# Banded attention by half tiles, and each V row's engine from a count of the work around its step

## The chip, the cores and the metric

The kernel runs on one core of a Trainium2 chip. The metric is the device time of one execution in microseconds (us). A measurement of before is a median of three executions.

## What is computed

One layer of a streaming encoder on 1024 tokens of width 1024, in float32: a norm, one input projection, two token mixers in parallel (gated linear attention; attention in a sliding band with sinks and distance slopes), their gated sum and projection, then a retrieval layer with product keys, a gated per-layer embedding, and a last norm. The two parts that the change touches are these:

```python
CHUNK = 64; SWA_WINDOW = 128          # a chunk of queries sees its own chunk and the one before
def swa_branch(q, k, v, sinks):
    ...
    logits = jnp.einsum('bnqhgd,bnkhd->bnhgqk', qc, kb).astype(f32) * (SWA_HEAD_DIM ** -0.5)
    ...
    dist = jnp.abs((W - 1) * CHUNK + qi[:, None] - kj[None, :]).astype(f32)
    logits = logits - slopes[:, :, None, None] * dist
    ...
    probs = jax.nn.softmax(jnp.concatenate([logits, sink], axis=-1), axis=-1)[..., :-1]
    out = jnp.einsum('bnhgqk,bnkhd->bnqhgd', probs.astype(v.dtype), vb)

def peer_ffn(h, w_q, sub_keys, u_tab, v_tab):
    ...   # for each token and each of 8 heads: the 16 best of 16384 experts, and their gates
        u = jnp.take(u_tab, e, axis=0)
        act = jax.nn.gelu(jnp.einsum('td,thkd->thk', xt, u).astype(f32))
        vv = jnp.take(v_tab, e, axis=0)
        return jnp.einsum('thk,thkd->td', (g * act).astype(xt.dtype), vv)
```

## The kernel before

**Rows.** Tokens lie in 8 tiles of 128. For each tile, head and rank one "row" of the retrieval layer is one indirect gather by GpSimd (L554): for 128 tokens the expert's u and v vectors, side by side, 8 KB a token, 1 MB in all. There are 1024 rows, and `uv` is a ring of ten. VectorE multiplies the u half with the token (`dot`, L1303, into `dots`), ScalarE makes the gelu (L1039) and the weight (L1044), and then the v half is added to the tile's sum, in one of two ways. Either VectorE does it (`add_row`, L1331, into `acc`), or ScalarE writes the weights as a diagonal matrix (`diagonal`, L1053, three buffers) and TensorE adds the row in PSUM by matmuls of 512 columns (L789, into `ysum`). `IS_PE` says which. Before, it holds a fixed pattern for each tile: every third row of a head's 16 for tiles 0 and 1, every second for tiles 2 to 5, three of four for tiles 6 and 7. The first six rows of a tile and the last four of all are VectorE's. GpSimd issues the gather of a row when the row ten before it is used, by the one engine or the other.

**Steps.** A step is two rows; there are 512 in which gathers are used (0 to 511), and negative ones for the opening. In step n VectorE does the dots of step n and two pieces of the top-k of a later head, then its rows of step n - 1. ScalarE makes the weights of step n - 1 and the diagonals of step n - 2, and TensorE adds its rows of step n - 2.

**Stages.** All the rest is cut into stages, which `plan()` puts on steps, for five segments of 1, 1, 2, 2 and 2 tiles: `gk`, `gv`, `gq`, `gr`, `sk`, `sv`, `sq` (projections), `la`, `u0`, `o0`, `t0` (linear attention), `lg`, `ex`, `va` (banded attention), `bgg`, `glo`, `bgs`, `swo`, `wo` (gates and output), `wq1` to `wq8` (queries and key search), and a tail `T0` to `T2` for finished tiles. Most of them begin with a weight slab of 1 MB, of which three fit; its matmuls (L597, L607) are a "piece". Each engine runs its own program in order: TensorE does a stage in its step, ScalarE and VectorE in the next. In a step TensorE does its due rows ahead of the stage. TensorE's results go through two PSUM banks that ScalarE empties (`copied`, L822), and TensorE waits for a bank to be emptied before it fills it again.

**Banded attention.** A batch is one tile with two groups of four heads (8 heads); a tile has two. `lg` multiplies 128 queries with 192 keys (three chunks, of which each query may see two, L646); VectorE adds slope times distance, where the table `dist` has 1e33 for keys that a query may not see, and takes the maximum (`biased`, L1120, L1124). `ex` has ScalarE's exponentials (L865) and VectorE's division (L1137). In `va` TensorE turns the probabilities, padded to 256 columns, in blocks of 128 (L660), ScalarE copies them out, and TensorE multiplies with V of two blocks (L666).

## Time and profile before

| | us |
|---|---|
| median of 3 executions | 3538.31 |
| lowest, highest | 3530.22, 3539.45 |
| the profiled execution, its time | 3534.93 |
| its span | 3533.1 |
| TensorE busy (share of the span) | 2829.1 (80%) |
| VectorE busy | 2572.2 (73%) |
| ScalarE busy | 1409.4 (40%) |
| GpSimd busy | 1287.0 (36%) |

In the profile PE is TensorE, PEld its weight loads, DVE VectorE, ACT ScalarE, POOL GpSimd and SP SyncE. The page shows the span in 40 equal slices: a digit is a busy share in tenths, GB/s is what the DMA engines moved. A row of the view by windows reads: from and to (us), length, busy time of PE, PEld, DVE, ACT and POOL (each with its number of instructions), the granted clock of TensorE as a share of 2.4 GHz, the DMA engines' mean busy share, and GB/s. The chain of waits is the work that ended last, followed back; a row is start, length, engine, what it wrote and its line. A matmul in float32 is two records, a transpose one.

### The profile page before, as it was taken

How to read it: one execution, taken by the hardware profiler on the slowest of the kernel's cores; microseconds unless marked ns; L12 is line 12 of the kernel's file. 1: busy time of each engine (PE TensorE's matmuls, PEld its weight loads, DVE VectorE, ACT ScalarE, POOL GpSimd, SP SyncE). 2: the span in 40 equal slices, each digit the busy share in tenths (PEclk: the TensorE clock that was granted, in tenths of full speed). 3: DMA queues.
4: the chain of work that ended last, by engine and by line, in shares of the span. 5: the costliest groups of instructions: out<-in, count | busy, mean ns of one | idle time of the engine just before them, and what ended most of it. 6: DMA issues, size and time to landing. Idle time of an engine off the chain costs nothing.

```text
span 3533.1 us, 35079 instructions
## 1 busy us (share of the span) xinstructions
PE 2829.1 (80%) x11044; PEld 1910.4 (54%) x11044; DVE 2572.2 (73%) x5366; ACT 1409.4 (40%) x3568; POOL 1287.0 (36%) x1028
## 2 busy tenths in 40 slices
PE   8889788987787997777876879978895978657665
PEld 7777566755565865444544637655473635213223
DVE  0247668798878868888777996787768885776664
ACT  2324543434433343444333443444534335334332
POOL 0012233343433244444442443343333433544441
PEclk9999899999998999898987989989998989879887
DMA  6589899999999999999999999999999999999995
GB/s 239 171 313 420 355 416 421 421 401 391 371 405 404 375 390 421 421 416 417 421 421 377 422 409 421 419 419 398 375 406 419 417 390 383 420 421 421 421 422 216
DMA packets 195915, 1376.57 MB, mean 390 GB/s; under 512 B 22401, under 2 KB 24321, under 8 KB 32018
## 3 DMA queue, kind: packets, MB, share of 16 engines
q0 software_dynamic: 147456, 1073.81, 74.0%
q1 hardware_dynamic: 48274, 300.51, 21.4%
q8 instruction: 90, 1.47, 0.2%
q14 instruction: 95, 0.78, 0.1%
HBM read 1363.22 MB, written 11.01 MB: 389 GB/s over the span
## 4 chain that ended last, share of the span: by engine, by line
PE 38%; DMA 28%; DVE 16%; issue 8%; ACT 6%; POOL 2%; DVEq 0%; POOLq 0%; SPq 0%; ACTq 0%
DMA uv<-in_uv,idx 24%; PE bank L597 14%; PE bank L607 10%; PE ysum L789 8%; DVE acc L1331 4%; DVE uv L1303 4%; DMA slab<-in_slabs 3%; POOL uv L554 2%; PE bank L666 2%; DVE lidx L1156 1%; DVE vals L1153 1%; ACT bufX L865 1%; DMA out<-bufA 1%; PE bank L660 1%; DVE bufE L1150 1%
## 5 line engine op out<-in xcount | busy, mean ns | idle before, releaser
L554 POOL DMA_INDIRECT uv<-in_uv,idx x1024 | 1286.8, 1257 | 2189.3 <-PE ysum L789 1004.4
L1303 DVE SCALAR_TENSOR_TENSOR uv<-uv,hbuf 128x1024 f32<-128x1024 f32 x1024 | 1244.8, 1220 | 420.5 <-DMA uv<-in_uv,idx 402.2
L789 PE MATMUL ysum<-uv,diag 128*128 128x512 f32 x2004 | 1059.1, 670 | 417.4 <-ACT diag L1053 412.2
L789 PEld LDWEIGHTS ysum<-uv,diag 128*128 128x128 f32 x2004 | 405.3, 212 | 937.0 <-ACT diag L1053 524.2
L1331 DVE SCALAR_TENSOR_TENSOR acc<-uv,dots,acc 128x1024 f32<-128x1024 f32 x523 | 668.9, 1279 | 107.8 <-ACT dots L1044 91.5
L1039 ACT ACTIVATE dots<-dots 128x2 f32<-128x2 f32 x512 | 102.9, 201 | 1017.2 <-DVE uv L1303 1011.5
L597 PE MATMUL bank<-bufA,slab 128*128 128x256 f32 (+1 forms) x2400 | 440.3, 343 | 14.3 <-DMA slab<-in_slabs 11.0
L597 PEld LDWEIGHTS bank<-bufA,slab 128*128 128x128 f32 x2400 | 391.4, 195 | 84.4 <-issue 32.9
L607 PE MATMUL bank<-slab,bufA 128*128 128x256 f32 x1408 | 317.7, 385 | 7.3 <-DMA slab<-in_slabs 4.7
L607 PEld LDWEIGHTS bank<-slab,bufA 128*128 128x128 f32 x1408 | 270.3, 193 | 61.3 <-issue 17.6
L597 PE MATMUL bank<-bufC,slab 128*128 128x256 f32 (+1 forms) x1280 | 245.0, 353 | 28.7 <-DMA slab<-in_slabs 14.2
L597 PEld LDWEIGHTS bank<-bufC,slab 128*128 128x128 f32 x1280 | 217.8, 204 | 71.1 <-issue 44.6
L1044 ACT ACTIVATE dots<-dots,gexp 128x1 f32<-128x1 f32 x1024 | 245.9, 287 | 20.6
L1039 ACT ACT_TABLE_LOAD x160 | 205.3, 1283 | 2.8
L1053 ACT ACTIVATE diag<-ident,dots 128x128 f32<-128x128 f32 x501 | 192.7, 395 | 11.9 <-PE ysum L789 5.5
L822 ACT ACTIVATE bufE<-bank 128x512 f32<-128x512 f32 (+1 forms) x136 | 69.6, 519 | 299.1 <-PE bank L597 272.0
L607 PE MATMUL bank<-slab,bufC 128*128 128x256 f32 x512 | 118.4, 391 | 15.4 <-DMA slab<-in_slabs 10.0
L666 PE MATMUL bank<-bufX,sv 128*64 128x512 f32 x128 | 81.8, 773 | 59.1 <-ACT bufX L822 59.1
L597 PE MATMUL bank<-bufQ,slab 128*128 128x256 f32 (+1 forms) x640 | 117.5, 343 | 4.0 <-DMA slab<-in_slabs 4.0
L607 PEld LDWEIGHTS bank<-slab,bufC 128*128 128x128 f32 x512 | 99.7, 196 | 37.9 <-DMA slab<-in_slabs 13.3
L607 PE MATMUL bank<-slab,bufQ 128*128 128x256 f32 x512 | 115.7, 385 | 2.2 <-ACT bufE L822 1.5
L597 PE MATMUL bank<-bufB,slab 128*128 128x256 f32 (+1 forms) x640 | 116.6, 341 | 0.0
(146 smaller groups left out, 2425.7 us busy)
## 6 DMA issues: line engine op xcount, KB each, us to landing
slab<-in_slabs SPq DMA_DIRECT2D x255, 1024.0 KB
uv<-in_uv,idx POOLq DMA_INDIRECT x1024
x_d<-acc SPq DMA_DIRECT2D x7, 512.0 KB
bufA<-in_x SPq DMA_DIRECT2D x3, 1024.0 KB, 11.8
bufA<-x_d SPq DMA_DIRECT2D x3, 1024.0 KB
out<-bufA SPq DMA_DIRECT2D x3, 1024.0 KB, 12.1
bufE<-in_g_ffn SPq DMA_DIRECT2D x5, 512.0 KB, 9.5
bufX<-in_g_fin SPq DMA_DIRECT2D x5, 512.0 KB
```

Source lines behind the costliest of these rows:

```text
L554: nc.gpsimd.indirect_dma_start(out=uv[:, at % NS, :], out_offset=None, in_=a["uv"], in_offset=bass.IndirectOffsetOnAxis(ap=idx[:, g % 4, k ...
L597: m = mm(o, w[:, k, g * P:g * P + P], src(k), start=(k == 0), stop=(k == KT - 1))
L607: m = mm(b[:, c0:c0 + PW], src[:, k, t * P:t * P + P], w[:, k, :], start=(k == 0), stop=(k == KT - 1))
L660: m = nc.tensor.transpose(b[:, c0:c0 + P], probs[:, GROUP * e + 2 * half + j, blk * P:blk * P + P], ident[:])
L666: m = mm(b[r0:r0 + HD, :], sv[:, t + blk, g * HD:g * HD + HD], pT[:, :, blk, :], start=(blk == 0), stop=(blk == 1))
L789: ins = mm(ysum[:, c, :], diag[:, m % DS, :], uv[:, at % NS, D + c * 512:D + c * 512 + 512], start=(m == first), stop=(m == last))
L822: fn(dst, src, kw.pop("func", ACT.Copy), **kw).then_inc(emptied, 1)
L1039: fn(part, part, ACT.Gelu_apprx_tanh).then_inc(gelu_done, 1)
L1044: m = fn(dots[:, g % 3, k:k + 1], dots[:, g % 3, k:k + 1], ACT.Copy, scale=gexp[:, g % 4, k:k + 1])
L1053: fn(diag[:, m % DS, :], ident[:], ACT.Copy, scale=dots[:, g % 3, k:k + 1]).then_inc(diag_done, 1)
L1303: v.scalar_tensor_tensor(out=row, in0=row, scalar=1.0, in1=hbuf[:, i % HB, :], op0=ALU.mult, op1=ALU.mult, accum_out=dots[:, g % 3, k:k + ...
L1331: v.scalar_tensor_tensor(out=row, in0=uv[:, at % NS, D:2 * D], scalar=dots[:, g % 3, k:k + 1], in1=row, op0=ALU.mult, op1=ALU.add).then_in ...
```

## The change

`BAND` becomes two chunks. In `lg` each half of a tile (64 queries) gets its own 128 keys, so a head is two matmuls of 64 rows by 128 columns, and no key is outside the band but for the first tile's missing chunk. Probabilities are 8 blocks of 128 columns without padding, so a head is one transpose and not two, and a group's turned probabilities take one bank and not two. V is held twice: `sv` as before, and `sv0` shifted by a chunk, which ScalarE fills with two more copies when it empties the bank of stage `sv`. `values` multiplies the first half's queries with `sv0` and the second half's with `sv`, 256 columns each, where two matmuls of 512 columns were summed up.

`IS_PE` comes from `shared_rows()`. It goes through the steps with a count for TensorE and one for VectorE, in a unit of its own: each is lowered by a step's pace (385, and 190 for a slab), raised by the stages' work from a table, and a row goes to the engine whose count is the lower with it. Rows of TensorE's are 586 after and 501 before; by tile 30, 56, 72, 78, 68, 66, 104, 112 after, and 38, 38, 61, 61, 61, 61, 92, 89 before. The plan of the stages is the same.

```diff
-BAND = 3 * CHUNK
+BAND = 2 * CHUNK
...
-ON_PE = [SOME, SOME, ODD, ODD, ODD, ODD, MOST, MOST]
...
-IS_PE = [at % TOPK in ON_PE[at // (NH * TOPK)] and at % (NH * TOPK) >= SPARE and at < ROWS - 4
-         for at in range(ROWS)]
...
+def work(s, n):
+
+    tt = tiles_in(s, n)
+    kind = n.rstrip("0123456789")
+    scores = kind == "wq" and n != "wq0"
+    pe = {"pp": 270 * tt, "hT": 95 * tt, "hb": 95 * tt, "T1": 200 * tt, "ga": 170 * tt + 100, "la": 75 * tt, "u": 270,
+          "o": 270, "t": 170 + 270 * (n[-1] != str(tt - 1)), "lg": 220, "va": 400}.get(kind, 0)
+    if n in PIECES and n != "pp":
+        pe += 535 if tt > 1 else 280 if kind in ("gk", "gv", "gr", "wo", "pg", "sv") else 345
+    dve = {"ga": 50 * tt, "la": 50 * tt, "u": 300, "o": 165, "t": 300 * (n[-1] != str(tt - 1)), "lg": 300, "ex": 120,
+           "glo": 30 * tt, "swo": 60 * tt, "rt": 110 * tt, "mx": 155 * tt}.get(kind, 0)
+    if n in ("wo3", "T2"):
+        dve += 100 * tt
+    return pe + 45 * tt * scores, dve + 230 * tt * scores
+
+
+def shared_rows():
+
+    found = []
+    pe = dve = 0
+    for n in range(END):
+        now, last = AT_STEP.get(n, []), AT_STEP.get(n - 1, [])
+        pace = 385 + 190 * sum(name in PIECES for _, name in now)
+        pe = max(pe - pace, 0) + sum(work(*stage)[0] for stage in now)
+        dve = max(dve - pace, 0) + 260 + sum(work(*stage)[1] for stage in last)
+        for at in (2 * n, 2 * n + 1):
+            may = at % (NH * TOPK) >= SPARE and at < ROWS - 4
+            found.append(may and pe + 135 < dve + 100)
+            if found[-1]:
+                pe += 135
+            else:
+                dve += 100
+    return found
...
     if n[:2] == "va":
-        return 6
+        return 4
...
                     for j in range(GROUP):
-                        o = wide[:, 2 * e + j // 2, (j % 2) * BAND:(j % 2) * BAND + BAND]
-                        m = mm(o, sqT[r0:r0 + HD, (g // 2) * GROUP + j, t * P:t * P + P],
-                               skT[r0:r0 + HD, g // 2, t * P:t * P + BAND], start=True, stop=True)
+                        for q0 in (0, CHUNK):
+                            m = mm(wide[q0:q0 + CHUNK, e, j * BAND:j * BAND + BAND],
+                                   sqT[r0:r0 + HD, (g // 2) * GROUP + j, t * P + q0:t * P + q0 + CHUNK],
+                                   skT[r0:r0 + HD, g // 2, t * P + q0:t * P + q0 + BAND], start=True, stop=True)
...
-                    for half in range(2):
-                        b = bank_for()
-                        for j in range(2):
-                            for blk in range(2):
-                                c0 = (2 * j + blk) * P
-                                m = nc.tensor.transpose(b[:, c0:c0 + P], probs[:, GROUP * e + 2 * half + j,
-                                                                              blk * P:blk * P + P], ident[:])
-                        m.then_inc(bank_full, 1)
+                    b = bank_for()
+                    for j in range(GROUP):
+                        m = nc.tensor.transpose(b[:, j * P:j * P + P], probs[:, GROUP * e + j, :], ident[:])
+                    m.then_inc(bank_full, 1)
                     pe.wait_ge(emptied, used.n)
-                    b = bank_for()
-                    for blk in range(2):
-                        m = mm(b[r0:r0 + HD, :], sv[:, t + blk, g * HD:g * HD + HD], pT[:, :, blk, :],
-                               start=(blk == 0), stop=(blk == 1))
+                    b = bank_for()[r0:r0 + HD, :].rearrange("p (j n) -> p j n", j=GROUP)
+                    for half, of in ((0, sv0), (1, sv)):
+                        q = slice(half * CHUNK, half * CHUNK + CHUNK)
+                        m = mm(b[:, :, q], of[:, t, g * HD:g * HD + HD], pT[:, :, q], start=True, stop=True)
                     m.then_inc(bank_full, 1)
...
                 elif n == "sv":
-                    rows(sv[:, 1:TT + 1, :], 0, tt)
+                    for ts in token_banks(tt):
+                        b = full()[:, 0:len(ts) * PW].rearrange("p (t n) -> p t n", t=len(ts))
+                        fn(sv0[0:CHUNK, ts[0] + 1:ts[-1] + 2, :], b[CHUNK:P], ACT.Copy)
+                        fn(sv0[CHUNK:P, ts[0]:ts[-1] + 1, :], b[0:CHUNK], ACT.Copy)
+                        copied(sv[:, ts[0]:ts[-1] + 1, :], b)
```

How it moves instructions shows in the listing of TensorE's program. The first place is the opening, tile 0's first batch: logits, two gates' pieces, then for each of two groups the transposes and the values. Before:

```order
L646 MATMUL wide<-skT,bufQ 128x192 x8
L597 MATMUL bank<-bufA,slab 128x128 x32
L660 MATMUL bank<-ident,bufX 128x128 x8
L666 MATMUL bank<-bufX,sv 64x512 x2
L660 MATMUL bank<-ident,bufX 128x128 x8
L666 MATMUL bank<-bufX,sv 64x512 x2
```

and after:

```order
L680 MATMUL wide<-skT,bufQ 64x128 x16
L631 MATMUL bank<-bufA,slab 128x128 x32
L692 MATMUL bank<-ident,bufX 128x128 x4
L698 MATMUL bank<-bufX,sv 64x4x64 x2
L692 MATMUL bank<-ident,bufX 128x128 x4
L698 MATMUL bank<-bufX,sv 64x4x64 x2
```

Twice as many logits of two thirds the columns; half the transposes; values of half the columns (the listing names `sv` for both copies of V).

The second place is segment 2, steps 80 to 84: a piece of `glo`, batch 1's values, a piece of a gate, batch 2's logits, and the V rows between them (`ysum<-uv,diag`, two matmuls a row). Before:

```order
L597 MATMUL bank<-bufB,slab 128x256 x16
L660 MATMUL bank<-ident,bufX 128x128 x8
L666 MATMUL bank<-bufX,sv 64x512 x2
L660 MATMUL bank<-ident,bufX 128x128 x8
L666 MATMUL bank<-bufX,sv 64x512 x2
L789 MATMUL ysum<-uv,diag 128x512 x2
L597 MATMUL bank<-bufA,slab 128x256 x16
L646 MATMUL wide<-skT,bufQ 128x192 x8
L789 MATMUL ysum<-uv,diag 128x512 x4
```

and after:

```order
L631 MATMUL bank<-bufB,slab 128x256 x16
L820 MATMUL ysum<-uv,diag 128x512 x4
L692 MATMUL bank<-ident,bufX 128x128 x4
L698 MATMUL bank<-bufX,sv 64x4x64 x2
L692 MATMUL bank<-ident,bufX 128x128 x4
L698 MATMUL bank<-bufX,sv 64x4x64 x2
L631 MATMUL bank<-bufA,slab 128x256 x16
L680 MATMUL wide<-skT,bufQ 64x128 x16
L820 MATMUL ysum<-uv,diag 128x512 x2
```

The row between the values and the gate's piece is gone, and two rows stand ahead of the values.

The third place is tile 6's part of the program, steps 407 to 411, with the tail of finished tiles: transposes (`T1`), then pieces of `pg`. Before:

```order
L586 MATMUL bank<-ident,bufB 128x128 x16
L789 MATMUL ysum<-uv,diag 128x512 x6
L607 MATMUL bank<-slab,bufQ 128x256 x16
L789 MATMUL ysum<-uv,diag 128x512 x6
L607 MATMUL bank<-slab,bufQ 128x256 x16
```

and after:

```order
L620 MATMUL bank<-ident,bufB 128x128 x16
L820 MATMUL ysum<-uv,diag 128x512 x8
L641 MATMUL bank<-slab,bufQ 128x256 x16
L820 MATMUL ysum<-uv,diag 128x512 x4
L641 MATMUL bank<-slab,bufQ 128x256 x16
```

Between two pieces stood three rows, and now two stand there.

## Rows read from the trace of the kernel before

**Rows 1.** The page: slices of DMA share and rate, and the gathers' queue.

```profile
DMA  6589899999999999999999999999999999999995
GB/s 239 171 313 420 355 416 421 421 401 391 371 405 404 375 390 421 421 416 417 421 421 377 422 409 421 419 419 398 375 406 419 417 390 383 420 421 421 421 422 216
...
q0 software_dynamic: 147456, 1073.81, 74.0%
```

**Rows 2.** The view by windows, the stretches of the span that the prediction counts.

```profile
90.00:146.00 56.00, 44.24 (x271) 32.83 (x270) 14.19 (x34) 23.96 (x61) 0.00 (x0) 0.88 0.38 130
146.00:249.00 103.00, 90.05 (x659) 84.57 (x658) 29.99 (x127) 25.20 (x59) 9.52 (x10) 0.93 0.77 277
...
371.00:431.00 60.00, 50.85 (x301) 37.18 (x302) 34.87 (x62) 28.47 (x67) 11.94 (x10) 0.86 0.82 325
431.00:737.00 306.00, 267.58 (x1311) 210.97 (x1310) 231.15 (x492) 123.46 (x291) 107.72 (x86) 0.94 1.01 420
737.00:1060.00 323.00, 262.92 (x1019) 184.18 (x1017) 269.47 (x474) 140.19 (x362) 123.87 (x96) 0.92 0.97 389
...
1138.00:1294.00 156.00, 143.69 (x588) 111.03 (x589) 121.68 (x304) 56.47 (x131) 49.20 (x40) 0.95 0.93 367
...
1900.00:2066.00 166.00, 137.48 (x508) 94.54 (x508) 150.97 (x433) 66.84 (x163) 66.46 (x55) 0.91 0.97 391
...
2390.00:2600.00 210.00, 183.03 (x674) 120.99 (x673) 158.21 (x295) 96.94 (x255) 74.49 (x63) 0.95 0.96 385
...
2830.00:3010.00 180.00, 144.16 (x425) 80.22 (x423) 126.24 (x277) 79.43 (x195) 73.24 (x58) 0.90 0.97 387
3010.00:3488.00 478.00, 312.50 (x608) 128.26 (x608) 328.17 (x608) 165.53 (x479) 216.38 (x174) 0.85 1.01 419
3488.00:3533.00 45.00, 19.14 (x74) 14.94 (x72) 12.80 (x14) 12.39 (x25) 0.00 (x0) 0.75 0.10 37
```

**Rows 3.** Who waited for whom at 871 to 880 us: total, times, longest.

```profile
DVE acc L1331 <- ACT dots L1044: 7.6, 1, 7.6
ACT L859 <- PE bank L597: 7.5, 1, 7.5
POOL uv L554 <- PE ysum L789: 7.4, 1, 7.4
```

**Rows 4.** The chain of waits, tile 0's first batch in the opening.

```profile
92.93 2.25 PE wide L646 x16
95.19 3.78 PE bank L597 x32
...
100.93 3.61 ACT bufX L865 x16
...
105.11 1.77 DVE bufX L1137
...
106.98 1.56 PE bank L660 x8
...
109.22 3.67 PE bank L666 x4
112.89 1.74 PE bank L660 x8
...
115.30 1.93 PE bank L666 x4
```

**Rows 5.** Groups by line, VectorE: dots, and rows into `acc`.

```profile
L1303 DVE SCALAR_TENSOR_TENSOR uv<-uv,hbuf 128x1024 f32<-128x1024 f32 x1024 | 1244.8, 1220 | 420.5 <-DMA uv<-in_uv,idx 402.2
...
L1331 DVE SCALAR_TENSOR_TENSOR acc<-uv,dots,acc 128x1024 f32<-128x1024 f32 x523 | 668.9, 1279 | 107.8 <-ACT dots L1044 91.5
```

**Rows 6.** The chain of waits: a row of TensorE's twice, and a piece.

```profile
385.07 1.72 PE ysum L789 x4
...
846.12 3.78 PE ysum L789 x4
...
2940.25 6.91 PE bank L607 x32
```

More of the change, by code:

```diff
@@ L180 @@
     AT_STEP.setdefault(_at, []).append((_s, _n))
+SPARE = 6
+def work(s, n):
[27 more added lines that the diff above has]
+    return found
+IS_PE = shared_rows()
+PE_UPTO, DVE_UPTO = [0], [0]
+for _at in range(ROWS):
+    PE_UPTO.append(PE_UPTO[-1] + IS_PE[_at])
+    DVE_UPTO.append(DVE_UPTO[-1] + (not IS_PE[_at]))
 def feature_banks(tt):
@@ L873, in window_out @@
                     r0 = (g % 2) * HD
[L874 to L876 removed]
+                    copied(pT, full().rearrange("p (j n) -> p j n", n=P))
                     copied(yswT[r0:r0 + HD, (g // 2) * GROUP:(g // 2) * GROUP + GROUP, t * P:t * P + P],
```

39 lines of the change are left out of this document (13 added, 26 removed).

## The prediction

> **What bounds the kernel now.** I read the page's slices first. From the fourth slice to the last but one the DMA engines are 80 to 100% busy and move 421 or 422 GB/s at the most, in 12 of the 40 slices just that [rows 1]. 74.0% of 16 engines' span is the 1024 gathers of expert rows [rows 1]; weight slabs are most of the rest. The change moves no byte of either (the table of distances alone shrinks, by 64 KB). So the kernel is bound by a transfer that it can't shorten, and what a change of the engines' work can give is only the time in which the transfer doesn't run at 421 GB/s.
>
> Next I cut the span into stretches and counted for each its length times (421 - GB/s)/421. At 431 to 737 us it is nothing (420 GB/s), at 3010 to 3488 us 2 us [rows 2]. What is left lies in three places. **The opening**, before gathers fill the engines, runs far below the rate up to 249 us, and 56 us of it, where tile 0's attention lies, at 130 GB/s [rows 2]. **Six stretches** in the middle lose 13.7 (371 to 431), 24.6 (737 to 1060), 20.0 (1138 to 1294), 11.8 (1900 to 2066), 18.0 (2390 to 2600) and 14.5 us (2830 to 3010), together 102.6 us [rows 2]. **The end**, 45 us after the last gathers at 37 GB/s [rows 2], holds tile 7's last norm and isn't touched.
>
> What makes a loss? The waits at 871 to 880 us show one whole [rows 3]: GpSimd waits 7.4 us for a row's matmul to free a slot of the ring of ten; VectorE waits 7.6 us for the weights that ScalarE makes; and ScalarE stands 7.5 us on a sigmoid, for TensorE to end the slab piece before it. Each engine runs its program in order, so a TensorE that is one piece late stops the other three, and the ring runs dry. Such a loss is a backlog of TensorE or VectorE in the steps with stages, larger than the ring's lead. A step's own budget is the transfer's: two rows are 2.1 MB, 5.0 us at 421 GB/s, and a slab adds 2.5 us.
>
> **The attention part.** The chain of the opening gives its prices, since there one batch (8 heads of a tile) stands on the chain link by link [rows 4].
> - Logits: 2.25 us for 16 records of 192 columns become 32 records of 128 columns in tiles of 64 rows by 64 columns. No row of before has that form. From above: 32 records of 128 columns in a slab piece took 3.78 us [rows 4], so +1.5. From below: if the two halves lay over each other, 1.9, so -0.35. I take +1.5, the form's nearest row. The Trainium skill (TensorE: Matmul & The Clock Gate, Part 3: Packing small matmuls) says that matmuls at different tile positions run at the same time; the two query halves differ in position, so by it the lower end would hold, and the sum below would be 4 us better in the opening. No run here shows such a pair yet.
> - Exponentials: eight in 3.61 us, each a third narrower. Between 0 and -1.2; I take -0.4, as most of an operation so short is fixed.
> - Normalizing: 1.77 us for 1536 elements, 1024 now: -0.6.
> - Transposes: half as many, 1.56 and 1.74 us: -1.65.
> - Values: columns halved, 3.67 (the low clock) and 1.93 us: -2.8. The eviction between transposes and values stays on the chain; the one that goes lay beside transposes.
> - Bias and maximum on VectorE become a third shorter too; they lie beside a gate's slab piece of 3.78 us. I count nothing; were that cover gone, 1.2 us more a batch.
>
> Sum: 3.95 us a batch on the chain, 7.9 us for the opening's two. Against it stand two more ScalarE copies where the V slab's bank is emptied (sv0's halves; TensorE's second next bank waits for them), under 1 us in the opening: I take 0.4. The opening gives **7.5 us**, with ends of 4 and 13. Since the gathers fill the DMA engines right behind it, nothing else can eat this.
>
> **The rows' engines.** A row costs VectorE 1.28 us and TensorE 1.72 at the full clock (3.4 for two), 3.78 at the low one [rows 5, 6]; a step's two dots cost VectorE 2.4 us [rows 5], and its top-k pieces are the same before and after. Before, TensorE has 501 of 1024 rows, dealt evenly within a tile; after, 586. The 85 that move take 109 us off VectorE and put 146 us on TensorE, neither of which is at its limit over the span, so the number matters little; where they lie does. In the listing of TensorE the piece, the row, the piece become the piece, the piece, and then four or eight matmuls of rows. With 2-tile pieces (6.91 us [rows 6]) and a row a step, TensorE needed 8.6 us of 7.5 in a stage step and 1.7 of 5.0 in an empty one; now 6.9 and 3.4. VectorE with both rows needs 5.0 of 7.5 and top-k, without them 2.4 of 5.0.
>
> Stretch by stretch, what of the loss goes:
> - 371 to 431: one-tile stages, two a step, two attention batches. The rows of steps 13 to 20 go from 5 on TensorE to 1 (7 us), and the batches give 8 us of chain. TensorE's lag here was its own work; of 13.7 I take **9**.
> - 737 to 1060: four batches, TensorE's rows 28 to 37 of 96. VectorE had 269.5 us busy of 323 [rows 2] with its bias, states and gates in bursts; it loses 9 rows (11.5 us) and 4 x 1.9 us of attention; the pairs now lie off the stages. Of 24.6 I take **16**.
> - 1138 to 1294: key search (two lists a tile) and the next segment's slabs together, no attention. TensorE is busy 143.7 of 156 us, VectorE 121.7 [rows 2]. There is no spare engine to move to: 16 rows become 15. Only the backlog that VectorE brings along from the steps ahead is smaller (7 of 20 rows on TensorE become 13). Of 20.0 I take **7**.
> - 1900 to 2066: the same search with tile 0's and 1's tail between; rows 24 to 32 of 54. Of 11.8 I take **6**.
> - 2390 to 2600: three batches, 12 us of chain. But rows run on TensorE two steps behind their gather, and here stages lie in two steps of three, so the pairs that were put on empty steps run in stage steps after all: 19 rows in its 13 steps with pieces, where 13 were. Of 18.0 I take **10**.
> - 2830 to 3010: tile 6, where 3 of 4 rows were TensorE's and its pieces came on top; Rows that run in a piece's step fall from 12 to 3 (15 us). Of 14.5 I take **11**.
>
> Together **59 of 102.6 us**; the ends are 25 and 98. Quiet stretches gain nothing: they run at the transfer's rate already.
>
> **The sum.** The profiled execution took 3534.9 us (its span 3533.1). 3534.9 - 7.5 - 59 = 3468.4. It lies 3.4 us under the median shown, so I forecast **3470 us**.
>
> **Rivals.**
> *The convoy stays.* The losses may come less from too much work than from the hand-overs (TensorE to ScalarE to VectorE and back), which the change leaves as they are, each batch still passing from engine to engine over six times. Then only the shorter batches count: some 25 us of the six stretches and the opening's 7.5: **3505**. For it: in [rows 3] nobody was overloaded within the 8 us themselves. Against: TensorE came late there after values that get shorter and a row that goes.
> *All stalls go.* If a loss needs a backlog over some threshold and the even load stays under it, 95 us go: **3435**. For it: 431 to 737 us, with as many stages a step, lost nothing. Against: the stretch at 1138.
> *The low clock (slower).* With pairs in every quiet step (166 of 178 rows at 3010 to 3488 us, 129 before) TensorE needs 3.4 us of 5.0 at 2.4 GHz, but 7.6 at 1.2 GHz [rows 6], where the transfer sets 5.0. The granted clock there is 0.85 on the mean [rows 2], so it spends about three tenths of the time at 1.2 GHz already. Each pair step held at 1.2 GHz with no slack left costs 2.6 us; there are 83. From 26 of them (67 us) the whole gain is eaten; half of them held give **3575**. For it: engines that pause between pairs are what rows show at the lower clock. Against: a TensorE that falls behind stops pausing, and in the stretches where it never paused the clock was full (2830 to 3010: 0.90; 371 to 431, with long waits, 0.86 [rows 2]); the ring's lead covers some steps. The Trainium skill names the same danger (TensorE: Matmul & The Clock Gate, table on what matters for kernels): idle gaps between bursts bring half the rate. By it the matmuls of a pair run slow; whether steps do is what the price above says.
> *It does not do what it says.* The planner's counts don't shift rows by the two steps at which TensorE runs them, so loads could rise where they should fall, and new stalls cancel the gain: **3530**.
>
> **How the numbers follow.** Forecast (3448 to 3490) 0.50; the convoy (3490 to 3520) 0.22; all stalls go 0.16; cancelled 0.06; the low clock 0.06. The range 3428 to 3512 leaves out the last two and the upper part of the second. A measurement can tell 0.3%, 11 us: faster than 3528 has 0.89, the same 0.05, slower 0.06.
>
> **What would show it.** Right: the first dot starts 7 to 8 us earlier; 371 to 431, 737 to 1060 and 2830 to 3010 at over 405 GB/s, 1138 to 1294 still under 400; values' matmuls half as long; a page with the same bytes. Wrong: waits of GpSimd for ysum of over 7 us in quiet stretches with the clock under 0.8 (the low clock), or the six stretches still losing over 70 us with engines less busy (the convoy).

## The result, and the profile after

| | us |
|---|---|
| after, median of 6 executions | 3510.7 |
| lowest, highest | 3507.9, 3518.2 |
| before, beside it | 3537.1 |
| after's profiled execution, its span | 3508.0, 3506.2 |

The change is faster by 0.7%: 0.993 of before, with a 95% interval of 0.991 to 0.994. That is 26 us where 67 were forecast. The time lies at the very end of the range (3512), near the rival "the convoy stays" (3505) and not at the forecast. That it lies inside at all is luck: it comes by a sum that neither the forecast nor a rival had.

The page of after (each engine's busy time, share and instructions; GB/s in 40 slices of the span; the gathers' queue with packets, MB and share):

```profile
PE 2874.4 (82%) x11512; PEld 1941.1 (55%) x11512; DVE 2458.6 (70%) x5276; ACT 1420.2 (41%) x3631; POOL 1236.4 (35%) x1028
...
GB/s 240 200 315 414 372 417 421 421 410 413 401 401 403 397 421 421 421 408 408 421 421 344 422 382 421 421 421 400 418 416 407 408 389 393 421 421 421 421 421 214
...
q0 software_dynamic: 147456, 1073.81, 74.3%
```

Against [rows 1] the bytes are the same, and the shape too: the same full stretches, the same dips. Some dips are shallower (401 to 403 where 371 to 375 stood) and one is deeper (344 where 377 stood). VectorE lost 114 us of work and TensorE gained 45, as the moved rows and the smaller attention make it. Busy time says little here: the transfer sets the pace.

To compare like with like, the spans are cut at the first dot of the same steps, not at the same microseconds, and the loss of each stretch is counted as the prediction does: length times (421 - GB/s)/421. The view by windows of after, so cut, with the columns of [rows 2]; the steps are 0 to 20, 63 to 110, 111 to 143, 144 to 242, 243 to 275, 323 to 356, 357 to 392, 393 to 421, and the quiet ones from 422:

```profile
243.00:420.00 177.00, 138.95 (x929) 116.38 (x927) 131.26 (x266) 84.45 (x199) 49.95 (x39) 0.91 0.96 393
...
728.00:1041.00 313.00, 259.13 (x1066) 184.32 (x1065) 251.61 (x463) 137.33 (x362) 120.91 (x95) 0.90 0.99 405
1041.00:1268.00 227.00, 212.80 (x887) 160.21 (x886) 187.54 (x514) 94.63 (x217) 79.53 (x66) 0.97 0.99 404
1268.00:1850.00 582.00, 481.04 (x1689) 300.60 (x1688) 433.95 (x823) 237.94 (x657) 245.51 (x201) 0.93 1.01 417
1850.00:2066.00 216.00, 169.46 (x573) 107.74 (x572) 175.04 (x499) 86.03 (x212) 77.32 (x66) 0.90 0.93 374
...
2361.00:2564.00 203.00, 176.12 (x704) 119.02 (x704) 164.23 (x310) 94.28 (x255) 78.36 (x66) 0.92 1.00 410
2564.00:2807.00 243.00, 198.88 (x742) 141.90 (x743) 184.57 (x471) 90.50 (x223) 82.73 (x73) 0.90 1.00 410
2807.00:2983.00 176.00, 139.84 (x407) 77.55 (x406) 126.50 (x275) 79.60 (x194) 71.68 (x60) 0.90 0.96 391
2983.00:3456.00 473.00, 344.11 (x744) 143.83 (x744) 283.79 (x567) 175.76 (x512) 191.26 (x173) 0.93 1.01 421
```

The same table for before and for the kernels of the experiments, in us of loss (each from the profiled execution of its kernel):

| steps | before | after | att_only | rows_only | t1_undo | t1_pairs | search_old | mix | mix2 | ring9 | shifted | lag1 |
|---|---|---|---|---|---|---|---|---|---|---|---|---|
| 0-20 | 13.9 | 11.8 | 9.7 | 23.5 | 14.0 | 9.2 | 15.0 | 9.3 | 10.2 | 21.2 | 14.1 | 3.4 |
| 21-62 | 0.7 | 0.7 | 0.0 | 1.5 | 0.7 | 0.0 | 2.2 | 3.6 | 0.0 | 2.2 | 0.7 | 0.0 |
| 63-110 | 24.6 | 11.9 | 20.5 | 15.8 | 9.6 | 15.6 | 10.3 | 10.4 | 7.9 | 17.2 | 17.1 | 19.2 |
| 111-143 | 19.3 | 9.2 | 23.1 | 9.2 | 9.2 | 19.2 | 9.2 | 7.5 | 9.4 | 14.5 | 10.0 | 15.0 |
| 144-242 | 1.4 | 5.5 | 1.4 | 14.0 | 6.9 | 0.0 | 5.5 | 2.8 | 4.2 | 14.0 | 11.2 | 36.0 |
| 243-275 | 11.7 | 24.1 | 12.7 | 22.0 | 18.6 | 16.5 | 10.4 | 12.7 | 12.2 | 27.8 | 9.5 | 18.6 |
| 276-322 | 0.0 | 0.0 | 1.4 | 0.0 | 0.0 | 2.1 | 0.0 | 0.7 | 0.7 | 0.7 | 2.1 | 0.0 |
| 323-356 | 18.3 | 5.3 | 7.0 | 13.0 | 6.3 | 7.6 | 6.3 | 3.5 | 6.5 | 10.5 | 5.3 | 18.6 |
| 357-392 | 1.1 | 6.3 | 0.5 | 11.7 | 5.8 | 2.8 | 2.8 | 1.1 | 2.8 | 14.9 | 5.2 | 16.2 |
| 393-421 | 14.4 | 12.5 | 15.2 | 11.6 | 14.7 | 16.2 | 14.2 | 14.1 | 10.2 | 18.8 | 8.0 | 33.7 |
| sum | 105.3 | 87.4 | 91.6 | 122.2 | 85.8 | 89.1 | 76.1 | 65.6 | 64.0 | 141.9 | 83.2 | 160.7 |

After against before: 23 us go at steps 63 to 143 and 13 at 323 to 356, but 12 come at 243 to 275, 4 at 144 to 242 and 5 at 357 to 392. So more than half of what went in one place came back in another. The row of before for steps 243 to 275, against that of after above (1850 to 2066 us):

```profile
1883.00:2088.00 205.00, 153.66 (x527) 99.42 (x525) 188.23 (x513) 82.14 (x200) 82.62 (x65) 0.84 0.98 397
```

A caution for all that follows: stretches whose program is the same in two kernels still differ by up to 5 us (steps 63 to 110: 20.5 and 15.6 in att_only and t1_pairs), and att_only's profiled execution (3511.4) was the slowest of its own, 8.5 us above its median. Medians decide between kernels; the table tells only where.

The opening went about as forecast in size. After's first dot starts at 243.0 us, before's at 249.4. In the profiles of all twelve kernels with the new attention it starts between 239.1 and 243.9, so the single 6.4 us stands for 5.5 to 10. The chain of waits of after, tile 0's first batch (start, us, what):

```profile
93.08 1.52 PE wide L680 x32
94.60 3.78 PE bank L631 x32
...
100.34 3.19 ACT bufX L896 x16
...
104.10 1.24 DVE bufX L1169
...
105.44 1.13 PE bank L692 x4
...
107.24 1.97 PE bank L698 x4
109.20 1.06 PE bank L692 x4
...
110.94 1.97 PE bank L698 x4
```

Held against [rows 4]: the logits took 0.7 us less, not 1.5 more (and less than the lower end, 0.35 less); exponentials 0.4 less; normalizing 0.5 less; the two lots of transposes 1.1 less; the values 1.7 less. From the first logit to the last value the batch went from 24.3 to 19.8 us.

### The profile page after: what moved, and what is told of

The parts are those of the page before. It is cut to its first block, busy times and chain, and to the rows that moved or that the text cites. A ratio compares the mean times of both kernels' runs of the same rounds, so it can differ in the third digit from the quotient of the medians.

```text
span 3506.2 us, 36073 instructions
## 1 busy us (share of the span) xinstructions
PE 2874.4 (82%) x11512; PEld 1941.1 (55%) x11512; DVE 2458.6 (70%) x5276; ACT 1420.2 (41%) x3631; POOL 1236.4 (35%) x1028
## 4 chain that ended last, share of the span: by engine, by line
PE 38%; DMA 33%; DVE 13%; ACT 7%; issue 6%; POOL 2%; DVEq 0%; SPq 0%; ACTq 0%; POOLq 0%
DMA uv<-in_uv,idx 28%; PE bank L631 14%; PE ysum L820 12%; PE bank L641 8%; DMA slab<-in_slabs 4%; DVE uv L1335 4%; DVE acc L1363 3%; POOL uv L588 2%; PE bank L698 1%; DVE lidx L1188 1%; DVE vals L1185 1%; ACT bufX L860 1%; ACT bufX L896 1%; ACT dots L1077 1%; PE bank L620 1%
## 5 line engine op out<-in xcount | busy, mean ns | idle before, releaser
L588 POOL DMA_INDIRECT uv<-in_uv,idx x1024 | 1236.2, 1207 | 2209.8 <-PE ysum L820 1335.8
L820 PE MATMUL ysum<-uv,diag 128*128 128x512 f32 x2344 | 1155.0, 640 | 342.1 <-ACT diag L1086 330.8
L820 PEld LDWEIGHTS ysum<-uv,diag 128*128 128x128 f32 x2344 | 462.3, 204 | 928.3 <-issue 500.7
L1363 DVE SCALAR_TENSOR_TENSOR acc<-uv,dots,acc 128x1024 f32<-128x1024 f32 x438 | 561.1, 1281 | 73.4 <-ACT dots L1077 51.4
L641 PE MATMUL bank<-slab,bufA 128*128 128x256 f32 x1408 | 322.8, 390 | 11.9 <-ACT bufA L882 6.2
L631 PE MATMUL bank<-bufC,slab 128*128 128x256 f32 (+1 forms) x1280 | 241.2, 350 | 14.1 <-ACT bufA L882 6.7
L1086 ACT ACTIVATE diag<-ident,dots 128x128 f32<-128x128 f32 x586 | 211.3, 394 | 49.6 <-PE ysum L820 41.8
L853 ACT ACTIVATE bufE<-bank 128x512 f32<-128x512 f32 (+1 forms) x136 | 69.8, 519 | 318.0 <-PE bank L631 279.2
L641 PE MATMUL bank<-slab,bufC 128*128 128x256 f32 x512 | 123.0, 402 | 27.2 <-DMA slab<-in_slabs 14.5
L631 PE MATMUL bank<-bufQ,slab 128*128 128x256 f32 (+1 forms) x640 | 119.3, 346 | 14.4 <-DMA slab<-in_slabs 13.8
L631 PEld LDWEIGHTS bank<-bufQ,slab 128*128 128x128 f32 x640 | 104.9, 195 | 30.9 <-DMA slab<-in_slabs 16.0
## 6 DMA issues: line engine op xcount, KB each, us to landing
out<-bufA SPq DMA_DIRECT2D x3, 1024.0 KB, 11.7
```

What stands on the lines that cost most here:

```text
L588: nc.gpsimd.indirect_dma_start(out=uv[:, at % NS, :], out_offset=None, in_=a["uv"], in_offset=bass.IndirectOffsetOnAxis(ap=idx[:, g % 4, k ...
L631: m = mm(o, w[:, k, g * P:g * P + P], src(k), start=(k == 0), stop=(k == KT - 1))
L641: m = mm(b[:, c0:c0 + PW], src[:, k, t * P:t * P + P], w[:, k, :], start=(k == 0), stop=(k == KT - 1))
L820: ins = mm(ysum[:, c, :], diag[:, m % DS, :], uv[:, at % NS, D + c * 512:D + c * 512 + 512], start=(m == first), stop=(m == last))
L853: fn(dst, src, kw.pop("func", ACT.Copy), **kw).then_inc(emptied, 1)
L1086: fn(diag[:, m % DS, :], ident[:], ACT.Copy, scale=dots[:, g % 3, k:k + 1]).then_inc(diag_done, 1)
```

## Experiments

All kernels compute the whole layer. Edits are against after unless it says otherwise. Differences in us are between medians. Before was measured again beside each group: 3535.4 beside att_only, rows_only, diag6 and search_old, 3536.2 beside lag1, att_lag1, shifted and mix, 3537.7 beside t1_undo, t1_pairs, ring9 and mix2, against 3537.1 beside after. So a difference of a few us between two groups says little; the ratios, given with their 95% intervals, are each to the before beside them.

**Halves of the change: att_only and rows_only.** The first has the new attention with the old rows, the second the old attention with the new rows:

```diff
-IS_PE = shared_rows()
+IS_PE = [at % TOPK in ON_PE[at // (NH * TOPK)] and at % (NH * TOPK) >= SPARE and at < ROWS - 4
+         for at in range(ROWS)]
```

> The new attention with the old fixed shares of rows (501 on TensorE). Theory A (the gain is the shorter batches; the new shares give back what they win, because a row of TensorE's is freed a step later than one of VectorE's): 3537 less the opening's 6 us and some 15 to 25 us of the six stretches, 3506 to 3516, so as fast as the whole change (3511) or faster. Rival B (the shares bring half of the gain and more): 3520 to 3530.

> The old attention with the new shares, the same rows on the same engines as in the changed kernel (586). Theory A: little, 3530 to 3545; the loss of steps 247 to 252 and 379, which grew with the change, shows here as well (7 us and 4 us more than before), the steps 335 to 343 get better. Rival B: 3515 to 3522.

att_only: 3502.9 us, 0.991 (0.990 to 0.993). rows_only: 3547.8 us, 1.003 (1.002 to 1.005). The attention alone is worth 34 us (32.5 against the before beside it), more than the whole change; the rows alone make the kernel 11 to 12 us slower. Each lies some 3 us outside what theory A said, and rival B is out. Put on the new attention the new shares cost 8 us by the medians and 6 by the ratios; the two intervals, 0.990 to 0.993 and 0.991 to 0.994, overlap, so that they cost this much is likely and not certain. That they don't bring half of the gain is clear. The table shows that they are not bad everywhere: against att_only, after loses 23 us less at steps 63 to 143 and 21 more at 144 to 275 and 357 to 392. In those last an even load doesn't help, and the next experiments ask what the rows do there.

**Is it the diagonals' buffers? diag6.** In the whole of after, among the waits, stands ScalarE's for a free diagonal, of which the ring has three, beside the ones that it could feed (total, times, longest):

```profile
POOL uv L588 <- PE ysum L820: 1335.8, 443, 21.2
POOL uv L588 <- DVE acc L1363: 500.3, 123, 26.7
...
PE ysum L820 <- ACT diag L1086: 330.8, 120, 16.9
...
ACT diag L1086 <- PE ysum L820: 41.8, 45, 2.4
```

```diff
-DS = 3
+DS = 6
```

> The changed kernel with six buffers for the diagonal weights in place of three. In the changed kernel ScalarE waits 42 us for TensorE to free one (5.5 us before), in its program order ahead of all that TensorE and VectorE wait for. Theory D (this new wait is where the gain went): 10 to 25 us faster, 3485 to 3500. Rival A: those waits lie where TensorE is the late one anyway; within 4 us of 3511, and the ScalarE wait gone from the profile.

3507.0 us, 0.992 (0.991 to 0.993): 4 under after, the intervals overlap. The wait is gone from the trace, and the one of TensorE for diagonals stays as it was:

```profile
PE ysum L820 <- ACT diag L1086: 338.6, 121, 16.8
```

So the 42 us of waiting cost 4 us at the most; theory D fell.

**Do rows free the ring too late? lag1 and att_lag1.** A row that TensorE has holds its slot of the ring two steps, one of VectorE's one step. lag1 runs TensorE's rows a step earlier; att_lag1 is the same edit on att_only:

```diff
-                rows_due += [at for at in (2 * (n - 2), 2 * (n - 2) + 1) if 0 <= at < ROWS and IS_PE[at]]
+                rows_due += [at for at in (2 * (n - 1), 2 * (n - 1) + 1) if 0 <= at < ROWS and IS_PE[at]]
...
-                for at in (2 * (n - 2), 2 * (n - 2) + 1):
-                    if 0 <= at < ROWS and IS_PE[at]:
-                        diagonal(at)
                 if 0 <= n - 1 < END:
                     weights(n - 1)
+                for at in (2 * (n - 1), 2 * (n - 1) + 1):
+                    if 0 <= at < ROWS and IS_PE[at]:
+                        diagonal(at)
```

> The changed kernel with TensorE's rows a step earlier: ScalarE makes a step's diagonals right behind its weights, and TensorE adds them ahead of the next stage. Theory A's price (a row of TensorE's holds its place in the ring a step longer than one of VectorE's, and a pair holds two): 10 to 20 us faster, 3490 to 3500, less lost in steps 243 to 254 and 371 to 392. Rival (TensorE then waits for weights ahead of its stages, so pieces come later): 3520 to 3560, with TensorE's wait for diagonals grown.

> The same step earlier with the old shares and the new attention (3503 without it). Theory A: less gain than with the pairs, 3495 to 3503. Rival: slower by as much as with the new shares.

lag1: 3581.0 us, 1.013 (1.011 to 1.014), 70 us above after. att_lag1: 3525.9 us, 0.997 (0.996 to 0.998), 23 above att_only. The waits of lag1 over its span:

```profile
PE ysum L820 <- ACT diag L1086: 463.1, 208, 17.5
ACT bufE L853 <- PE bank L631: 407.2, 74, 12.7
```

Both grew, by 132 us (120 to 208 times) and, from 279.2 us in 64, by 128. The earlier row waits for its weight, and since TensorE's program is in order, the stage's piece behind the row waits with it, and ScalarE for the piece. That is the rival's account, though the loss is larger than it said (3520 to 3560), and smaller in att_lag1 than "as much as with the new shares". Over the whole kernel a row's place in TensorE's order outweighs the step that its slot is held longer. But the slot isn't free of charge: in steps 243 to 254, where theory A foretold less loss, lag1 loses 7.5 us where after loses 15.9. At 371 to 392 it loses 10.6 against 5.7.

**Is it the search stretches? search_old.** After with the old rows at the steps where the key search runs and its neighbours, 243 to 275 and 371 to 413:

```diff
+for _n in (*range(243, 276), *range(371, 414)):
+    for _at in (2 * _n, 2 * _n + 1):
+        IS_PE[_at] = WAS_PE[_at]
```

> The changed kernel with the old pattern of rows in steps 243 to 275 and 371 to 413 alone, where key search and the tail of finished tiles lie between each other and the new pairs stand in runs. Theory A (pairs there make the new losses, 8.7 to 15.9 us in steps 246 to 254 and 0.8 to 5.7 in 379 to 392): 10 to 15 us faster, about 3498. Rival (they come from what stands ahead of these steps, VectorE's or ScalarE's order): 3508 to 3515.

3490.6 us, 0.987 (0.986 to 0.989), 20 us under after. The new shares of 76 steps cost 20 us: in the table 13.7 of them lie at 243 to 275 and 3.5 at 357 to 392. The forecast of 10 to 15 was too small.

**Does the planner count in the wrong steps? shifted.** TensorE's rows of step n run among the stages of step n + 2, VectorE's one step after their dots. `shifted` counts them there:

```diff
-        pe = max(pe - pace, 0) + sum(work(*stage)[0] for stage in now)
-        dve = max(dve - pace, 0) + 260 + sum(work(*stage)[1] for stage in last)
+        pe = max(pe - pace(n + 2), 0) + sum(work(*stage)[0] for stage in AT_STEP.get(n + 2, []))
+        dve = max(dve - pace(n + 1), 0) + 260 + sum(work(*stage)[1] for stage in AT_STEP.get(n, []))
```

> The changed kernel with its planner's counts shifted to the steps in which the rows really run (TensorE two steps on, VectorE one); 536 rows on TensorE in place of 586. If the missing shift is what spoils the new shares: 3490 or faster, and less lost in steps 243 to 254. If the number and the pairing of the rows spoil them: 3500 to 3512.

3501.5 us, 0.990 (0.989 to 0.991), 9 us under after and, within the noise, no better than the old shares (3502.9). Both halves of what was expected came in part: the time is the second's, but the loss of steps 243 to 254 fell from 15.9 us to 5.7, below that of any other kernel here. What it wins there (9.5 against 24.1 at 243 to 275) it gives back in part at 63 to 110 (17.1 against 11.9) and 144 to 242 (11.2 against 5.5). So the missing shift is a real fault, and at 243 to 275 most of the matter, as far as its 50 rows fewer on TensorE don't have a part in it.

**What queues behind one wait? t1_undo and t1_pairs.** One place where the listings of TensorE's programs differ at 243 to 254 and at 371 to 392 is behind `T1`, the tail's transposes, which wait for ScalarE. TensorE's part of the timeline (start, us, what; in brackets its idle time before and for whom), steps 246 to 249 of after:

```profile
1884.73 3.60 PE L820 MATMUL ysum<-uv,diag 128*128 128x512 f32 x8
1897.05 4.02 PE L620 MATMUL bank<-ident,bufB 128*128 128x128 f32 x16 [8.72 <-ACT bufB L1047]
1900.85 8.11 PE L820 MATMUL ysum<-uv,diag 128*128 128x512 f32 x16
1908.80 7.07 PE L631 MATMUL bank<-bufC,slab 128*128 128x256 f32 x32
```

and of att_only:

```profile
1910.30 4.02 PE L628 MATMUL bank<-ident,bufB 128*128 128x128 f32 x16 [8.71 <-ACT bufB L1055]
1914.11 3.69 PE L828 MATMUL ysum<-uv,diag 128*128 128x512 f32 x8
1917.63 7.07 PE L639 MATMUL bank<-bufC,slab 128*128 128x256 f32 x32
```

Both wait the same 8.7 us, in which the steps run on for the other engines. Then after has four rows (16 records) to catch up before the slab piece, att_only two. Who waited meanwhile, in after from 1874 to 1925 us:

```profile
POOL uv L588 <- PE ysum L820: 44.3, 10, 12.1
ACT bufE L853 <- PE bank L631: 15.6, 2, 8.0
DVE vals L1185 <- ACT bufE L853: 12.4, 2, 6.4
```

and in the answering 51 us of att_only (1887 to 1938):

```profile
POOL uv L596 <- PE ysum L828: 18.1, 4, 6.3
ACT bufE L861 <- PE bank L639: 13.9, 2, 7.6
POOL uv L596 <- DVE acc L1371: 13.6, 4, 6.0
```

GpSimd, whose gathers are the transfer, waits 44.3 us for slots of the ring, all of TensorE's rows, where it waited 31.7, 18.1 of them for TensorE's. t1_undo gives back two of the four rows at each of the two `T1` places (4 rows of 1024); t1_pairs is the mirror, four rows at those places in att_only:

```diff
+for _n in (247, 248, 375, 376):
+    IS_PE[2 * _n], IS_PE[2 * _n + 1] = False, True
```

> The changed kernel with four rows of 1024 given back from TensorE to VectorE: the first of the two rows in steps 247, 248, 375 and 376. These stand in TensorE's program right behind the transposes of stage T1, on whose input it waits 9 to 11 us, and ahead of the next key-search piece. Theory T (a wait of TensorE's ahead of rows costs by the rows that queue behind it: 16 matmuls, 7.0 us, where 8, 3.7 us, stood before, and all engines wait for the piece behind them): the loss of steps 243 to 254 falls from 16 to about 10, that of 371 to 392 from 6 to about 1, and the time by 8 to 12 us, to about 3500. Rival (the sheer number of TensorE's rows in these stretches): under 3 us.

> The mirror: the new attention with the old shares (3503), and the same four rows given to TensorE. Theory T: the losses of 243 to 254 and 371 to 392 grow by 3 to 5 us each; 3508 to 3513. Rival: under 2 us.

t1_undo: 3504.7 us, 0.990 (0.989 to 0.992), 6 under after (9 by the ratios). t1_pairs: 3510.7 us, 0.992 (0.991 to 0.994), 8 above att_only, but 5.5 if each is taken against the before beside it, and 3.5 by the ratios. Both went the way the queue says, though each pair of intervals overlaps, so the times alone don't show it; t1_undo's 6 us lie between the two theories' bounds. The place itself, steps 243 to 254 in the windows of after, t1_undo, att_only and t1_pairs, in this order:

```profile
1849.00:1934.00 85.00, 62.22 (x202) 38.96 (x201) 59.98 (x184) 33.56 (x84) 24.47 (x23) 0.84 0.88 342
```

```profile
1849.00:1931.00 82.00, 59.15 (x196) 37.76 (x195) 62.82 (x186) 32.80 (x82) 26.26 (x24) 0.83 0.92 360
```

```profile
1868.00:1944.00 76.00, 54.80 (x193) 36.55 (x192) 64.31 (x188) 30.50 (x75) 26.53 (x23) 0.83 0.93 367
```

```profile
1860.00:1940.00 80.00, 58.72 (x202) 38.15 (x201) 61.94 (x186) 31.21 (x77) 26.35 (x23) 0.84 0.89 352
```

The losses are 16.0, 11.9, 9.7 and 13.1 us: two rows more behind this wait go with 3 to 4 us more of loss, about what TensorE is busy with them (3.69 us for 8 records). The other kernels bear it out when the loss is counted in just the three steps of `T1`, the rows behind it and the piece (249 to 251, and 377 to 379 at the second place):

| kernel | rows behind `T1` | loss 249-251 | loss 377-379 |
|---|---|---|---|
| before | 2 | 6.3 | 0.8 |
| att_only | 2 | 6.5 | 0.0 |
| mix | 2 | 6.3 | 0.6 |
| mix2 | 2 | 6.7 | 2.2 |
| search_old | 2 | 6.1 | 0.8 |
| t1_undo | 2 | 6.0 | 3.5 |
| shifted | 2 | 5.8 | 3.5 |
| t1_pairs | 4 | 8.3 | 2.1 |
| after | 4 | 8.8 | 5.1 |
| diag6 | 4 | 9.0 | 6.7 |
| rows_only | 4 | 8.7 | 7.0 |
| lag1 | 4 | 5.8 | 4.5 |

(att_lag1, with two rows of other steps there, loses 4.2 and 0.0, and ring9, with a slot less and four rows, 9.4 and 8.5.) At the first place seven kernels with two rows lose 5.8 to 6.7 us, and four kernels with four rows 8.3 to 9.0: some 2.5 us for two rows. At the second the paired kernels say 1.6 (t1_undo) and 2.1 (t1_pairs), and more of the growth comes from elsewhere. The exception is lag1. Its four rows stand behind the same kind of wait,

```profile
1928.64 4.01 PE L620 MATMUL bank<-ident,bufB 128*128 128x128 f32 x16 [7.45 <-ACT bufB L1047]
1932.45 7.12 PE L820 MATMUL ysum<-uv,diag 128*128 128x512 f32 x16
```

and at the first place they cost nothing more. They are the rows of steps 248 and 249, where after's are those of 247 and 248, so each holds its slot a step less. So the length of the queue isn't all. That the late rows hold slots which GpSimd needs fits better, and so do the waits of t1_undo from 1874 to 1925 us:

```profile
POOL uv L592 <- PE ysum L824: 34.7, 7, 11.0
```

That is 9.6 us less than in after, while ScalarE's and VectorE's waits for the piece and what follows it are as before (15.5 and 12.4 us). That the later piece costs something too isn't ruled out; no run separates the two.

The whole growth in steps 243 to 254 is 6.3 us from att_only to after. The rows behind `T1` are some 2.5 of it directly. Most of the rest lies ahead of that wait: steps 243 to 248 lose 6.1 us in after, 1.7 to 5.0 in the kernels with the old shares there, and nothing in shifted and lag1. It was not taken apart, nor was the growth of the other stretches.

**Does a delay count only beyond the ring? ring9.** The ring of gathers with one slot less, in after:

```diff
-NS = 10
+NS = 9
```

> The changed kernel with a ring of nine rows in place of ten. Both theories say that a loss is the part of a late engine's delay that the ring's lead does not cover; one row is 2.5 us of lead, and the changed kernel has some 20 places that lose: 30 to 60 us slower, 3540 to 3570. If the losses were not the ring's (the slabs', say): under 10 us.

3560.0 us, 1.005 (1.004 to 1.007), 49 us above after; the loss grows from 87.4 to 141.9, in nearly every stretch with stages and none from step 422 on. One slot is 2.5 us of transfer. So a loss is what a delay has over the ring's lead. That it is single delays, and not a stretch's sum of work, that the ring covers or doesn't fits this, but this run can't tell the two apart.

**The shares where they help: mix and mix2.** mix takes the new shares at steps 60 to 143 and 414 to 423 and the old ones elsewhere (519 rows of TensorE's); mix2 takes, besides, those of shifted at 93 to 110 and 384 to 423 (511):

```diff
+for _n in (*range(0, 60), *range(144, 414), *range(424, END)):
+    for _at in (2 * _n, 2 * _n + 1):
+        IS_PE[_at] = WAS_PE[_at]
+for _n in (*range(93, 111), *range(384, 424)):
+    for _at in (2 * _n, 2 * _n + 1):
+        IS_PE[_at] = SHIFTED[_at]
```

(The last three lines are mix2's alone.)

> The new attention; the new shares in steps 60 to 143 and 414 to 423 alone, where the traces so far lose less with them (121 to 143: 9 us against 23 with the old shares; 414 to 421: 0 against 5), and the old pattern everywhere else. If the stretches add up: 3503 (new attention, old shares) less 14, less 5, less 5 to 8 of steps 63 to 110: 3476 to 3482. If losses only move to the next stretch (the rival: what one stretch wins, its neighbour gives back): 3495 or more.

> The mixed shares (3487) with those of the shifted planner in steps 93 to 110 and 384 to 423, where it lost 0 us against 8, and 3, 4 and 2 against 7, 1 and 6. If losses of stretches add up: 8 to 12 us less, 3475 to 3479. If each stretch depends on what stands ahead: 3483 to 3490.

mix: 3486.7 us, 0.986 (0.984 to 0.987), between the two theories. mix2: 3483.5 us, 0.984 (0.983 to 0.985), its executions from 3479.2 to 3484.2: what was expected if a stretch depends on what stands ahead of it. Gains of single stretches, picked out of single profiles, add up only in part; steps 93 to 110, where shifted lost nothing, lose 3.8 us in mix2. The 3 us between mix and mix2 are within the noise. mix2 is 27 us faster than after and 54 faster than before.

## Why the prediction was wrong, step by step

**In one sentence.** The step that failed is the term of 34 us for the rows' engines, that taking work off an engine in a stretch gives that work back as time. Measured, the new shares give 14 to 23 us at steps 63 to 143, lose about as much at 144 to 275 and 357 to 392, and cost 6 to 8 us in sum.

**What bounds the kernel: right.** In the quiet steps of all kernels the transfer runs at 420 or 421 GB/s, and the rest of the time is the opening, the losses and the end. From the two profiled executions: the opening gave 6.4 us (first dot), the table's losses 17.9, the end and rounding 2.6: together the 26.9 between 3534.9 and 3508.0.

**The opening: right in size, in part by luck.** It gave 6.4 us for 7.5. Per batch the terms sum to 4.5 us where 3.95 were taken, but three were off and cancelled: logits by 2.2 us one way, values and transposes by 1.1 and 0.5 the other. The logits: the upper bound was taken, +1.5, from the nearest row of the same width; it was -0.7, beyond the lower end (-0.35). 32 records of 128 columns took 1.52 us in tiles of 64 by 64 against 3.78 in full tiles. The Trainium skill (TensorE: Matmul & The Clock Gate, Part 3: Packing small matmuls) says that such tiles run at the same time; the trace agrees, and the end of the range that it pointed to was the better value. The values: -2.8 was taken and -1.7 measured. The first group halved, 3.67 to 1.97; the second stayed, 1.93 to 1.97, though its columns halved. So 4 records of 256 columns now take what 4 of 512 took for the second group before. TensorE's granted clock tells why, in the windows of before (which hold the second group, from 115.3 us) and of after (from 110.9 us):

```profile
113.00:118.00 5.00, 4.31 (x19) 2.64 (x20) 0.00 (x0) 2.31 (x4) 0.00 (x0) 0.87 0.01 3
```

```profile
110.00:113.00 3.00, 2.31 (x7) 0.91 (x6) 0.00 (x0) 0.66 (x2) 0.00 (x0) 0.50 0.03 5
```

Before, the granted clock was 0.87 on the mean by then, so mostly at its full level of 2.4 GHz, after a first group of 3.67 us. After, it is still 0.50, which is 1.2 GHz. That the shorter bursts with the same waits between them are what keeps it there is likely, but no run shows it by itself.

**The attention in the six stretches: right in size.** The convoy rival put it at some 25 us; att_only's median gives 34 in all, of which the opening is 6.4 (after's first dot) to 8.9 (its own, at 240.5 us): 25 to 28 for the stretches. Its column of the table shows only 14 us of difference; that execution was 8.5 us above its median.

**The rows' engines: the step that failed.** Of the 59 us, 34 were to come from the shares (59 less those 25). They cost 8 by the medians, 6 by the ratios. The prediction read a loss as a surplus of one engine's work over a step's budget and credited each row that left a stage step with its busy time. By stretch:

| stretch (steps) | forecast | after | att_only |
|---|---|---|---|
| 371-431 (0-20) | 9 | 2.1 | 4.2 |
| 737-1060 (63-110) | 16 | 12.7 | 4.1 |
| 1138-1294 (111-143) | 7 | 10.1 | -3.8 |
| 1900-2066 (243-275) | 6 | -12.4 | -1.0 |
| 2390-2600 (323-356) | 10 | 13.0 | 11.3 |
| 2830-3010 (393-421) | 11 | 1.9 | -0.8 |
| the others | 0 | -9.3 | -0.1 |

(The two last columns are before's loss less the kernel's, from the table. The last row joins 21 to 62, 144 to 242, 276 to 322 and 357 to 392.)

Where all engines are loaded without long waits the credit was earned: 63 to 143 gave 22.8 of the 23 forecast, and it is the shares that gave most of it: att_only has 0.3 there, and t1_pairs, which is the same up to step 246, 9.1. Where the search and the tail run, TensorE's time isn't short in sum (169.5 us busy of 216 at 243 to 275): it stands and waits for ScalarE, 8.7 us at a time, and what counts is which rows are queued behind the wait, and how long they hold their slots. There the planner put two rows in each of two steps (247, which is empty, and 248, whose own stage is `T1`); both run behind `T1`'s wait, since TensorE adds a row two steps after its gather, and TensorE had 8.11 us of rows to do before the next piece. The experiments show this for some 2.5 us at the first place and 2 at the second; most of the 21 us that the shares lose elsewhere (against att_only) is shown to come from them, by att_only and search_old, but not by which wait. The prediction saw the shift at 2390 to 2600 ("pairs that were put on empty steps run in stage steps after all"), took it for a small loss of gain, and did not ask at 1900 to 2066 what stands ahead of those pairs. The other thing it left out: "quiet stretches gain nothing" is true as said, but they could lose. At 144 to 242 and 357 to 392, where before lost 1.4 and 1.1 us, after loses 5.5 and 6.3, and rows_only 14.0 and 11.7.

**At 371 to 431 and 2830 to 3010** the reason was wrong in another way: by the listings the rows in tile 6's piece steps fell from 12 to 3 as said, and the loss stayed (14.4 to 12.5). So it wasn't TensorE's surplus that made it. mix2 and shifted, with shares counted in the right steps, have 10.2 and 8.0 there; what makes the rest was not found. At 371 to 431 (here steps 0 to 20) the forecast was 9 and 2.1 came; why was not looked into.

**The rivals.** *The convoy stays* (3505) is the nearest in time, and its sign came: the six stretches, as the table cuts them, still lose 74.8 us in after (of the signs of being right, 393 to 421 stayed at 391 GB/s, under 405). But it comes by another sum: the attention gave the 25 us of the stretches, and beside that the shares won 28 us in some places and lost 24 in others (after against att_only, by the table; by the medians they lost 8 in all). The rival had the shares do nothing. *All stalls go* is out. *It does not do what it says*: half right; the missing shift is there, loads rose where it said they could, and counting it in gives 9 us (shifted). *The low clock* is refuted, and with its sign turned. (Its "the clock was full" at 2830 to 3010 was misread: [rows 2] has 0.90 there, and TensorE busy for 144 of 180 us, so it did pause.) In the quiet steps from 422 on the granted clock of after is 0.93 (the last row of its windows), with before's at 0.85 [rows 2]. That of att_only, in which steps with one row and with two take turns, is at 0.84:

```profile
2986.00:3459.00 473.00, 316.61 (x601) 129.96 (x602) 325.03 (x604) 163.92 (x474) 217.58 (x174) 0.84 1.01 421
```

Each of the two takes 473 us at 421 GB/s, so neither clock costs anything there. TensorE runs two rows in each step in after, and often three in a row every second step in att_only. From 2990 to 3450 us it waits for ScalarE's diagonals 59 times in after, 121.6 us in all, and 55 times in att_only, 153.3 us. One run of rows of each, with the pause ahead of it:

```profile
3105.11 3.70 PE L820 MATMUL ysum<-uv,diag 128*128 128x512 f32 x8 [1.27 <-ACT diag L1086]
```

```profile
3108.35 7.11 PE L828 MATMUL ysum<-uv,diag 128*128 128x512 f32 x12 [2.82 <-ACT diag L1094]
```

The Trainium skill (TensorE: Matmul & The Clock Gate, the table on what matters for kernels) says that idle gaps between bursts bring half the rate. The trace agrees in kind: the kernel with the shorter gaps has the higher clock. The rival feared the pauses between pairs; they are shorter than those of the old shares.

**The chances.** The step from "an engine is overloaded here" to "taking work off it gives that work back" carried the forecast's 0.50, and [rows 3] spoke against it already: within those 8 us nobody was overloaded, each waited for the next.

## What to carry to other kernels

Where engines with in-order programs feed each other and a ring of transfers, don't move work by counts of each engine's load alone. Look for the instructions that wait for another engine, and keep short what stands behind them and holds slots of the ring. Count work in the step in which an engine really does it. Four rows instead of two behind one such wait went with 2.5 us more of loss in those three steps and 3 to 4 in the twelve around them, though the rows were 2 of 1024. Try an assignment stretch by stretch on the chip and keep it where it wins; here that gave 27 us over using it everywhere. And count a stretch that loses nothing now as one that can begin to.

## What the runs showed of the hardware

- Matmuls on 64 rows and 64 columns of the array lie over each other in float32. Here two that follow each other use the same rows and the other half of the columns. All logits of before, all of after, and all values of before and of after (busy us, mean ns of one):

```profile
L646 PE MATMUL wide<-skT,bufQ 64*128 64x192 f32 x256 | 39.2, 349 | 0.0
L680 PE MATMUL wide<-skT,bufQ 64*64 64x128 f32 x512 | 27.7, 292 | 0.0
L666 PE MATMUL bank<-bufX,sv 128*64 128x512 f32 x128 | 81.8, 773 | 59.1 <-ACT bufX L822 59.1
L698 PE MATMUL bank<-bufX,sv 128*64 128x256 f32 x128 | 47.6, 509 | 53.6 <-ACT bufX L853 53.6
```

512 records cover 27.7 us, 54 ns each, though one takes 292; before, 256 of 192 columns covered 39.2 us. A third fewer columns and twice the records made 29% less time.

- Half the columns is half the time at one clock only. The values went from 81.8 us (773 ns a record) to 47.6 (509 ns), 0.58 and not 0.5. At either level a group of four records was about halved, 3.67 to 1.97 us at 1.2 GHz and 1.93 to 1.08 at 2.4 GHz; but some groups are at the low clock now that were at the full one, as the second of the opening. Two groups of after:

```profile
847.44 1.08 PE L698 MATMUL bank<-bufX,sv 128*64 128x256 f32 x4 [0.69 <-ACT bufX L853]
927.91 1.97 PE L698 MATMUL bank<-bufX,sv 128*64 128x256 f32 x4 [8.04 <-ACT bufX L853]
```

The granted clock is 1.00 from 847 to 849 us, and 0.50 from 927 to 934.

- Two rows in every step kept TensorE's granted clock at 0.93 where one and two by turns had 0.84, over the same 473 us and at the same rate of transfer. They are also more rows (744 and 601 records of TensorE's in all), so the even spacing alone isn't shown to do it.
